# The last two thirds of a modulation product, moved from TensorE in head 0 to GpSimd in heads 0 to 3

## What is computed

```python
def modulation(cvec, w, b):
    mod = jax.nn.silu(cvec) @ w + b
    return jnp.split(mod[:, None, :], N_MOD, axis=-1)
    ...
sh_a, sc_a, g_a, sh_f, sc_f, g_f = modulation(c, ada_w[l], ada_b[l])
csh_a, csc_a, cg_a, csh_f, csc_f, cg_f = modulation(c_ctx[None, :], ada_w[l], ada_b[l])
    ...
x = x + g_a * y_lat
x = x + g_f * expert_choice_ffn(modulate(x, norm2_g[l], sh_f, sc_f), ...)
```

## Time and profile before

| | us |
|---|---|
| three runs | 2749.73, 2746.8, 2752.75 |
| median | 2749.73 |
| profiled execution, first to last instruction | 2752.9 |
| TensorE busy in it | 2667.6 (97%) |
| GpSimd busy in it | 170.4 (6%) |
| heads 1 to 7, each | about 76.4 |

### The profile page before, as it was taken

The page is one execution under the profiler, slowest core; times in us unless marked ns, Lnnn a source line. Parts: engine busy times, 40 slices in busy tenths (PEclk is TensorE's granted clock), DMA queues, the critical chain, the costliest instruction groups (busy, mean ns, idle before and its releaser), DMA issues.

```text
span 2752.9 us, 33182 instructions
## 1 busy us (share of the span) xinstructions
PE 2667.6 (97%) x13084; PEld 1873.1 (68%) x13084; DVE 1303.1 (47%) x2417; ACT 560.8 (20%) x942; POOL 170.4 (6%) x140
## 2 busy tenths in 40 slices
PE   6999999999899999999799999999999999999998
PEld 3788888887667666787443333334595877888887
DVE  4255665655465666645311111146473335654654
ACT  3121212222234344311111010122322113000001
POOL 0122211220000000232000000000000000000000
PEclk9999999999999999999899999999999999999999
DMA  9721212211111121235799999952103421233231
GB/s 334 236 62 53 61 43 56 61 30 38 39 47 54 54 62 42 82 90 178 281 409 409 409 409 409 409 178 61 31 1 87 132 73 47 77 92 92 80 89 46
DMA packets 328720, 374.66 MB, mean 136 GB/s; under 512 B 11073, under 2 KB 274070, under 8 KB 325270
## 3 DMA queue, kind: packets, MB, share of 16 engines
q1 hardware_dynamic: 328326, 371.93, 39.8%
q10 hardware_dynamic: 272, 1.05, 0.1%
HBM read 370.85 MB, written 2.10 MB: 135 GB/s over the span
## 4 chain that ended last, share of the span: by engine, by line
PE 89%; DVE 5%; DMA 2%; DVEq 1%; ACT 1%; issue 1%; SPq 0%; ACTq 0%; POOLq 0%; POOL 0%
PE psum L1782 29%; PE psum L2169 12%; PE psum L1462 7%; PE psum L2347 5%; PE psum L720 3%; PE psum L1129 2%; PE psum L2071 2%; PE psum L2026 2%; PE psum L815 2%; PE psum L728 2%; PE psum L2885 2%; PE psum L705 2%; PE psum L1318 2%; PE psum L1370 2%; PE psum L1347 2%; PE psum L2967 1%
## 5 line engine op out<-in xcount | busy, mean ns | idle before, releaser
L1782 PE MATMUL psum<-arena 128*128 128x256 f32 x4144 | 908.6, 378 | 1.9 <-DVEq L1805 1.1
L1782 PEld LDWEIGHTS psum<-arena 128*128 128x128 f32 x4144 | 777.8, 189 | 121.0 <-issue 10.0
L2169 PE MATMUL psum<-arena 128*64 128x512 f32 x1536 | 347.8, 597 | 5.1 <-DMA arena<-in_w_down 3.5
L2169 PEld LDWEIGHTS psum<-arena 128*64 128x64 f32 x1536 | 103.4, 136 | 220.8 <-issue 217.2
L1462 PE MATMUL psum<-arena 128*128 128x256 f32 x896 | 206.6, 381 | 0.0
L1462 PEld LDWEIGHTS psum<-arena 128*128 128x128 f32 x896 | 164.7, 189 | 32.5 <-issue 11.7
L1814 DVE TENSOR_TENSOR arena<-psum,arena 128x256 f32<-128x256 f32 x66 | 28.1, 425 | 303.0 <-ACT arena L1827 183.5
L2076 DVE SCALAR_TENSOR_TENSOR arena<-psum,arena 128x512 f32<-128x512 f32 x64 | 48.1, 751 | 233.0 <-PE psum L2071 232.5
L2347 PE MATMUL psum<-arena 128*128 128x512 f32 (+1 forms) x416 | 157.5, 536 | 0.0
L2347 PEld LDWEIGHTS psum<-arena 128*128 128x128 f32 x416 | 79.8, 193 | 75.1 <-issue 70.8
L1789 POOL TENSOR_TENSOR arena<-arena 128x512 f32<-128x512 f32 x34 | 47.3, 1392 | 1090.5 <-DMA arena<-in_w_in 631.3
(11 more groups left out here) (407 smaller groups left out, 3294.7 us busy)
## 6 DMA issues: line engine op xcount, KB each, us to landing
arena<-in_w_gate SPq DMA_DIRECT2D x64, 1024.0 KB, 18.4
arena<-in_w_up SPq DMA_DIRECT2D x64, 1024.0 KB, 18.4
arena<-in_w_down SPq DMA_DIRECT2D x64, 1024.0 KB, 18.4
arena<-in_w_in SPq DMA_DIRECT2D x120, 512.0 KB, 4.5
arena<-in_ada_w SPq DMA_DIRECT2D x24, 1024.0 KB, 7.3
arena<-in_w_up SPq DMA_DIRECT2D x32, 512.0 KB, 5.4
arena<-in_w_down SPq DMA_DIRECT2D x32, 512.0 KB, 5.2
arena<-in_w_out SPq DMA_DIRECT2D x16, 512.0 KB, 4.0
```

The costliest lines, as they stand in the source:

```text
L1782: mm = pe.matmul(psum[:, base + b, c * HALF:(c + 1) * HALF], w, v, start=(first and q == 0 and m in (0, 2, 3, 4)), stop=(last and q == KC ...
L2169: mm = pe.matmul(psum[64 * e:64 * e + 64, bank + n, :], tokens(e, 2 * q + k), w[:, k, 512 * n:512 * n + 512], start=(q == 0 and k == 0), s ...
```

## The change

TensorE multiplies no late tile any more. The 16 tiles are cut into 32 pieces of 128 x 1024 (512 KB), piece m being half m % 2 of row block k = m // 2 % 8 of part 1 + m // 16. GpSimd multiplies each piece by the column of silu_c for its k, one factor per partition, and adds the product to an accumulator of 128 x 2048; the first k of a part writes the accumulator without an addition. The accumulator of part 1 is stored in DRAM and read back at the end (SBUF has no room for both). The sum over the 128 partitions is left for TensorE: between head 3 and head 4 it multiplies both accumulators by ones. GpSimd's pieces stand behind its weight sums in its order, by the list LATE_AFTER: after the sums of (head, quad) 0-1: pieces 0 to 3, 0-2: 4 to 8, 1-0: 9 to 11, 1-1: 12 to 14, 1-2: 15 to 17, 2-0: 18 to 20, 2-1: 21 to 23, 2-2: 24 to 26, 3-0: 27 to 29, 3-1: 30 and 31. Their loads stand on SyncE's queue between weight units (LATE_BETWEEN), two buffers deep: the load of piece m waits until piece m - 2 has been added. The constants that were loaded behind the late tiles are now loaded ahead of them. The loops over heads 1 to 7 are cut in two at head 4 on TensorE and VectorE, and written out up to head 3 on SyncE and GpSimd; `mod_ready` is gone.

The core of the diff:

```diff
-        def sp_mod_late(sp):
+        def sp_late_first(sp):
+            sp_consts_late(sp)
             sp.wait_ge(sem("turn_out"), NT)
             sp.wait_ge(sem("vectors"), 2)
-            for n in range(2 * KC):
-                if n >= 3:
-                    sp.wait_ge(sem("late_used"), n - 2)
-                sp.dma_start(LATE[n % 3], ada[1 + n // KC, n % KC]).then_inc(ws.full[8 + n % 3], 16)
-            sp_consts_late(sp)
+            sp_late(sp, 0, 4)
+
+        def sp_late(sp, first, end):
+            for m in range(first, end):
+                r, k, half = m // (2 * KC), m // 2 % KC, m % 2
+                if m >= 2:
+                    sp.wait_ge(sem("late_used"), m - 1)
+                if m == 2 * KC + 1:
+                    sp.dma_start(late_store, late_acc).then_inc(ws.full[10], 16)
+                sp.dma_start(late_w[m % 2], ada[1 + r, k][:, 1024 * half:1024 * half + 1024])\
+                  .then_inc(ws.full[8 + m % 2], 16)
...
+        def pool_late(pool, first, end):
+            for m in range(first, end):
+                r, k, half = m // (2 * KC), m // 2 % KC, m % 2
+                acc = late_acc[:, 1024 * half:1024 * half + 1024]
+                pool.wait_ge(ws.full[8 + m % 2], 16 * (m // 2 + 1))
+                if m == 0:
+                    await_once(pool, "silu_c")
+                if m == 2 * KC:
+                    pool.wait_ge(ws.full[10], 16)
+                product = late_w[m % 2] if k else acc
+                pool.tensor_scalar(product, late_w[m % 2], silu_c[:, k, 0:1], None, ALU.mult)
+                pool.drain()
+                if k:
+                    pool.tensor_tensor(acc, acc, product, ALU.add)
+                    pool.drain()
+                pool.sem_inc(sem("late_used"), 1)
...
+        def pe_late_sums(pe, r):
+            if r == 1:
+                pe.wait_ge(ws.full[10], 32)
+            else:
+                pe.wait_ge(sem("late_used"), LATE_PIECES)
+            for j in range(4):
+                mm = pe.matmul(psum[32 * j:32 * j + 2, 3 + r, :], ones[:, 0:2], late_sum_of(r)[:, 512 * j:512 * j + 512],
+                               start=True, stop=True)
+            mm.then_inc(once(f"late_sums_{r}"), 1)
...
         def pool_hg(pool):
-            for g in (1, 2):
-                pool_hg_sums(pool, 0, g)
-            with pool.Fori(1, HEADS) as i:
+            for i in range(LATE_HEADS):
+                for g in range(3):
+                    if i or g:
+                        pool_hg_sums(pool, i, g)
+                        pool_late(pool, *LATE_AFTER[3 * i + g])
+            with pool.Fori(LATE_HEADS, HEADS) as i:
                 for g in range(3):
                     pool_hg_sums(pool, i, g)
+
+        LATE_AFTER = [(0, 0), (0, 4), (4, 9), (9, 12), (12, 15), (15, 18), (18, 21), (21, 24), (24, 27), (27, 30), (30, 32), (32, 32)]
+        LATE_BETWEEN = {7: sp_late_first, 31: sp_late_again}
+        for n_ in range(2, 11):
+            LATE_BETWEEN[2 * n_ + 5 + 2 * ((n_ - 2) // 3)] = lambda sp, at_=LATE_AFTER[n_]: sp_late(sp, *at_)
...
             pe_hg_plain(pe, 1)
-            late(0, 1)
-            pe_hg_gates(pe, 0, lambda: late(2, 3))
-            late(4, 5)
+            pe_hg_gates(pe, 0, lambda: None)
...
             pe.wait_ge(sem("head_values_out"), 2)
-            pe_mod_turn(pe, 1)
-            pe_mod_turn(pe, 2)
             pe.wait_ge(sem("consts_in"), 32)
-            with pe.Fori(1, HEADS) as i:
...
+            with pe.Fori(1, LATE_HEADS) as i:
+                pe_hg_head(pe, i)
+            for r in (1, 2):
+                pe_late_sums(pe, r)
+            for r in (1, 2):
+                pe_mod_turn(pe, r)
+            await_once(pe, "mod_done")
+            with pe.Fori(LATE_HEADS, HEADS) as i:
+                pe_hg_head(pe, i)
...
             dve_hg_quad(dve, 0, 2)
-            dve_mod_late(dve)
             dve_begin(dve, 1)
             dve.wait_ge(sem("consts_in"), 32)
-            with dve.Fori(1, HEADS) as i:
...
+            with dve.Fori(1, LATE_HEADS) as i:
+                dve_hg_head(dve, i)
+            dve_mod_late(dve)
+            with dve.Fori(LATE_HEADS, HEADS) as i:
+                dve_hg_head(dve, i)
```

More of the change, by code:

```diff
@@ L157, in phase, with load @@
         self.total += n * iters
-    def load(self, eng, name, then=None, between={}):
+    def load(self, eng, name, between={}, apart=1):
         ph = self.phases[name]
         n = len(ph["units"])
[L162 to L170, removed]
+        for i in range(apart):
+            for u, (src, dst, _, _) in enumerate(ph["units"]):
+                if i:
+                    eng.wait_ge(self.used, i * n + ph["again"][u])
+                else:
+                    wait(eng, self.used, ph["first"][u])
+                eng.dma_start(dst, src(i)).then_inc(self.full[ph["slots"][u]], 16)
+                if i * n + u in between:
+                    between[i * n + u](eng)
+        if ph["iters"] > apart:
+            with eng.Fori(apart, ph["iters"]) as i:
                 for u, (src, dst, _, _) in enumerate(ph["units"]):
@@ L279, in mixed_block_kernel @@
                             for u in range(KC)])
-        for n in range(2 * KC):
-            ws.count[8 + n % 3] += 16
+        for m in range(4 * KC):
+            ws.count[8 + m % 2] += 16
+        ws.count[10] += 32
         w_in1 = cut(A["w_in"][0], P)
@@ L432, in mixed_block_kernel @@
         mod_rows = Carve(arena, EXTRA[0] + S + KC * C + C, EXTRA[1]).take(2, 512)
-        LATE = [arena[:, at:at + 2048] for at in (BT_LO + 4096, BT_LO + 6144, BT_LO + 2048)]
+        late_acc = arena[:, BT_LO + 2048:BT_LO + 4096]
+        late_kept = arena[:, BT_LO + 4096 + 3 * S:BT_LO + 4096 + 7 * S]
+        late_w = [late_kept[:, 1024 * m:1024 * m + 1024] for m in range(2)]
+        late_store = nc.dram_tensor("late_store", (P, 2048), F32, kind="Internal").ap()
+        LATE_PIECES = 4 * KC
+        LATE_HEADS = 4
         def pe_mod_unit(pe, r, k, w):
@@ L495, in dve_mod @@
             dve.drain()
-            dve.sem_inc(sem("mod_ready"), 1)
         def dve_mod_late(dve):
@@ L508, in dve_mod_late @@
             dve.drain()
+            dve.sem_inc(once("mod_done"), 1)
         HALF = S // 2
@@ L1010, in dve_hg, with dve_hg_head @@
             dve_hg_quad(dve, 0, 2)
-            dve_mod_late(dve)
             dve_begin(dve, 1)
             dve.wait_ge(sem("consts_in"), 32)
-            with dve.Fori(1, HEADS) as i:
[L1015 to L1031, removed]
+            with dve.Fori(1, LATE_HEADS) as i:
[3 more added lines that the diff above has]
+                dve_hg_head(dve, i)
+        def dve_hg_head(dve, i):
+            dve_take(dve, i)
+            dve_level(dve, i, 0)
+            dve_level(dve, i, 1)
+            dve_hg_quad(dve, i, 0)
+            dve_level(dve, i, 2)
+            dve_conv1(dve, i)
+            dve_level(dve, i, 3)
+            dve_level(dve, i, 4)
+            dve_hg_quad(dve, i, 1)
+            dve_level(dve, i, 5)
+            dve_conv2(dve, i)
+            dve_level(dve, i, 6)
+            dve_level(dve, i, 7)
+            dve_hg_quad(dve, i, 2)
+            dve_states(dve, i)
+            dve_begin(dve, i + 1)
+            dve_readout(dve, i)
         PAIRS_Q = HEADS
```

78 lines of the change are left out of this document (38 added, 40 removed).

## The result

The kernel after takes 2780.73 us in the median of 4 runs (2780.18 to 2782.71), beside 2750.29 for the kernel before on the same chip (4 runs, 2746.8 to 2752.75). The ratio is 1.0114, with a 95% interval from 1.0102 to 1.0126, so it is slower by 30 us. The forecast was 2785, in a range from 2758 to 2815. The profiled execution has a span of 2779.1 and took 2780.93, which is on the median. With the same 1.8 between span and time, the profiled one of before (span 2752.9) would be a run of about 2754.7, an estimate 4.4 above its median. So the spans differ by only 26.2 where the medians differ by 30.4.

The account below looks back on a forecast made before the run. TensorE, busy 97%, was taken as the bound, with VectorE right behind it. The terms -17.2 + 35.8 + 8.0 + 8.5 = +35.1 on the span of 2752.9 gave 2788.0, a median of 2785, range 2758 to 2815.

Parts of the forecast that it names:

- Late tiles out of head 0, 17.2: TensorE's path in head 0 and start of head 1: 15.4 of late products and 1.8 more go, gain 17.2 us.
- The price of a piece, 3.3: On GpSimd: one multiplication at 1.1 and one addition at 2.2 make a piece of 3.3 us.
- A: GpSimd's addition of a piece's product to the accumulator, 1024 columns, priced as two sums at 2.2 us.
- T: GpSimd's multiplication of a piece by its factor (tensor_scalar), priced at 1.1 us, at most 2.2.
- GpSimd has room; its sums stay ahead of TensorE's quads, cost nothing.: GpSimd's queue: idle 28.3 and 31.6 in a head; sums have 13 and 19 us to spare, so no quad is delayed.
- the queue rival: Late pieces delay SyncE's weight units or GpSimd's sums, 4 to 10 in each of three heads: 2800 to 2820, chance 0.08.
- VectorE's delays, 35.8: Heads 1 to 3: VectorE's operations between SBUF areas alternate with GpSimd's, stalling TensorE by 35.8 us; bounds nothing and 50.
- only A excludes: Rival: T, with one input, leaves VectorE alone, only A shuts it out: 2771, with less clock 2767; chance 0.14.
- Between the loops, 8.0: Between heads 3 and 4 TensorE waits for the accumulators' sum, copies, transposes and additions: cost 8.0 us, 6 to 11.
- Clock, 8.5: Slower granted clock behind seven stalls of over 2.5 us, five counted at 1.7: cost 8.5 us, bounds 0 and 18.
- It gains: Rival: GpSimd's batches fall where VectorE has slack or gaps let it through: -9.2, 2740.5 us; chance 0.08.
- T costs like A: Rival: 13 multiplications cost 1.1 more each, plus clock: 2802 us; chance 0.15.

Follow-up runs that it names:

- without pieces: The change without GpSimd's multiplications and additions, except the first four multiplications; loads, waits and the stage between the loops stay: 2740.99 us, ratio 0.9969.
- the multiplications alone: The change with GpSimd's additions left out and all 32 multiplications kept: 2748.36 us, ratio 0.9993.
- the pieces on VectorE: From the kernel before: in head 0 VectorE does 24 half tiles by fused multiply and add, TensorE keeps 4 tiles, GpSimd gets none: 2741.41 us, ratio 0.9968.

## Why the prediction was right

The time was forecast within 5, and so was the sum of the changes. Part of that is luck: the stalls were priced 13.3 too high and the late sums 10.8 too low, and the two errors cancel.

*Late tiles out of head 0, 17.2.* No product of the late tiles is left there. The profiles without pieces and with the multiplications alone, which have no new wait in head 0, show 17.9. Right.

*The price of a piece, 3.3.* **This step failed.** A was priced at 2.2 and lasts 2.35. T was taken at 1.1, with an upper bound of 2.2 from "what a sum reads and writes", and lasts 2.84: here GpSimd's one-input operation with a factor per partition is slower than its two-input addition of the same size, and no row of before said so. A piece is 5.2, or 5.6 with its gaps. The 1.5 that was estimated from the Trainium skill (GPSIMD Engine Reference, "Elementwise — side-by-side cycle accounting") is too low as well; the measurement decides.

*"GpSimd has room; its sums stay ahead of TensorE's quads, cost nothing."* It failed by the same step. The nine pieces ahead of head 1's quad 0, with one quad's sums among them, ran from 54.50 to 106.30; 9 at 3.3 and the sums would have been 35 of these 52, and what the forecast named as the queue rival's mechanism came: 2.4 and 8.3 of waiting, in head 0, though slack had been read only in head 2. It also said that each quad's sums have at most one batch ahead of them, and gave no figure for the four and the five pieces of head 0. With 13 and 19 to spare in head 2, heads 2 and 3 hold even now. The rival itself had priced a miss in each of three heads at 2800 to 2820; one miss does not make that.

*VectorE's delays, 35.8.* The mechanism holds, and the takes of heads 2 and 3 as its places; the size is below: 9.8 in head 1 (forecast 11.6), 8.1 in head 2 (17.6), 4.6 in head 3 (6.6), 22.5 in all. In head 1 the places were wrong and the sum came out near by luck. The take there (107.22 to 115.43) was over while TensorE itself waited for the late sums, so level 1 waits for nothing instead of 6.0. The 6.15 stands ahead of level 4, where nothing was forecast: the pieces behind the sums of quad 1 came later than planned, and meet the convolution and the level's work. One A beside one of its operations:

```profile
151.04 2.37 POOL L497 TENSOR_TENSOR arena<-arena 128x1024 f32<-128x1024 f32 x1
151.12 2.56 DVE L910 TENSOR_TENSOR arena<-arena 128x256 f32<-128x256 f32 x1
```

The timeline of the change at head 2's take:

```profile
211.19 3.84 POOL L494 TENSOR_SCALAR arena<-arena 128x1024 f32<-128x1024 f32 x1 [0.20 <-issue]
211.45 0.95 DVE L889 COPY arena<-arena 128x1536 f32<-128x1536 f32 x1
212.32 1.79 DVE L890 COPY arena<-arena 128x1536 f32<-128x1536 f32 x1
214.03 1.41 DVE L891 COPY arena<-arena 128x768 f32<-128x768 f32 x1
215.18 2.46 POOL L497 TENSOR_TENSOR arena<-arena 128x1024 f32<-128x1024 f32 x1
215.36 2.56 DVE L892 COPY arena<-arena 128x512 f32<-128x512 f32 x1
```

L892 alone takes 2.56 where L833 of before took 0.42, behind the whole A; L890 (0.95 before) and L891 (0.56 before) are held once each within T. Three pieces turn by turn were forecast; around the longer T three copies get through, and the take is over after one piece, so level 1 waits 6.56, not 9.9. At levels 4 and 5 of head 2 1.4 is lost, not 7.7. There two-input operations meet T's free second part:

```profile
240.77 2.84 POOL L494 TENSOR_SCALAR arena<-arena 128x1024 f32<-128x1024 f32 x1 [0.20 <-issue]
241.32 0.84 DVE L909 TENSOR_TENSOR arena<-arena 128x256 f32<-128x256 f32 x1
242.08 0.41 DVE L910 TENSOR_TENSOR arena<-arena 128x256 f32<-128x256 f32 x1
```

That is half of the rival "only A excludes", for which the forecast had 2771: the experiments give T 7.4 and A 22.8.

*Between the loops, 8.0.* From the end of head 3's work to the next quad, 8.6 are lost, and 10.5 with clock by the kernel without pieces. Right, with its waits where they were put (L521 waits 3.45 for VectorE, and the quad behind it 1.30).

*Clock, 8.5.* The leftovers of the table add to 9.9. Right in size; but the stalls of over 2.5 are five and not seven, and one of them stands in head 0.

The terms as forecast add to +35.1. As measured they are -17.2, +10.8, +22.5, +8.6 and +9.9, so +34.6, and with -4.9 from the start-up, -0.4 in head 4's stretch and -3.2 regained later this is the span's 26.2, but for 0.1 of rounding. The late sums were missed through the price of T. The stalls were 13.3 too high mostly for another reason: each GpSimd operation was taken to hold off one VectorE operation for all of its own time, and T holds off the two-input ones for 1.0 only.

*Rivals.* "It gains", 2740.5, is what the kernel without pieces shows, at 2740.99: it needed that GpSimd's arithmetic disturb nobody, and it disturbs. "T costs like A" fails: T takes longer but holds for less.

## What to carry to other kernels

- Before work goes to an idle engine, ask what it shuts out: here 164 us of GpSimd work, in a change that takes 15 us off TensorE, cost 40 us through a VectorE without slack and through sums in GpSimd's own queue. Count the work's place, beside the tight operations or not, before its amount.
- Look first for idle time on an engine that does the work faster in a place where it has nothing tight: VectorE was busy for under 10 of 56 us in head 0, does a piece in 1.28 instead of 5.6, and the kernel gains 8.6 us.
- Where no row shows an operation, take its price from another one with a bound that is wide to the top, and ask what the queue does at that bound. From GpSimd's first piece (54.50) to the end of TensorE's query (104.73) are 50.2. At 3.3 a piece the nine pieces and one quad's sums fill 35 of them, and at 4.4, the forecast's bound, 45, with the next quad's sums of 5.3 still to come: at that bound the queue is full, and the term can't be put at nothing.

## What the hardware showed that was not expected

- GpSimd's one-input `tensor_scalar` of 128x1024 f32 takes 2.84 undisturbed (3.00 in the mean of 32, after), a two-input `tensor_tensor` of the same size 2.35, a fill 0.98 (mean of 140).
- The three shut VectorE out in different ways. The two-input one holds off a two-input operation for its whole time (0.41 became 2.04 to 2.56). `tensor_scalar` does so for its first 1.0 (0.41 became 0.84), but can hold off a copy later on (0.56 became 1.41 at 214.03 in the change). A fill leaves two-input operations alone (0.67 kept), but holds off copies between SBUF areas (0.95 became 1.78).
- VectorE's fused multiply and add of the same 1024 columns takes 1.28 (1.35 in the mean of 20), less than half of GpSimd's multiplication alone.
- At the same place of the program, 35 to 45 us, the granted clock was 0.50 in the profile of before, 0.66 in that with the pieces on VectorE, 0.83 without pieces, and 1.00 in the change. The wait for a load ahead of the place was 2.51 before and 1.50 after. This start-up is worth up to 5 us between two profiles. Before was profiled once, so whether the edits in head 0 play a part in it is not shown.
